# A four-block diffusion backbone on one core: feed-forward parts of 8, 8 and 6 blocks instead of 12 and 10, and a weight ring of four 8 KB slots instead of two of 12 KB

## What is computed

```python
FFN_HIDDEN = ((8 * D_MODEL // 3 + 255) // 256) * 256          # 2816 = 22 blocks of 128

def swiglu(h, w13, w2):
    a, b = jnp.split(h @ w13, 2, axis=-1)
    return (jax.nn.silu(a) * b) @ w2

silu_c = jax.nn.silu(c)
...
for i in range(DEPTH):
    ...
    mod_l = jnp.split((silu_c @ mod_w[i] + mod_b[i])[:, None, :], N_MOD, axis=-1)   # mod_w[i]: 1024 x 6144
    hl = modulate(rmsnorm(xl, mix_pre_g[i]), mod_l[0], mod_l[1])
    ...
```

## Time and profile before

| | |
|---|---|
| median of 3 runs | 2926.69 us (2925.06 to 2929.64) |
| span of the profiled execution | 2911.3 us |
| median less span (what lies around the span) | 15.4 us |
| PE busy | 2446.2 us, 84% |
| DVE, ACT, POOL busy | 1263.4, 773.5, 209.5 us |
| bytes moved | 305.42 MB, 105 GB/s over the span |
| mean granted clock of PE | 0.908 |

### The profile page before, as it was taken

How to read it: one execution, slowest core, us unless ns; L and a number is a source line. 1 busy time by engine, 2 the same in 40 slices (tenths; PEclk the granted TensorE clock), 3 DMA queues, 4 the chain that set the end, 5 groups by cost and what they waited for, 6 DMA issues and landing times.

```text
span 2911.3 us, 29789 instructions
## 1 busy us (share of the span) xinstructions
PE 2446.2 (84%) x12523; PEld 1820.3 (63%) x12523; DVE 1263.4 (43%) x1889; ACT 773.5 (27%) x1225; POOL 209.5 (7%) x167
## 2 busy tenths in 40 slices
PE   7897787999997998989999972617548799998998
PEld 3664463888882774537888821516347399764997
DVE  2333434332325564243313337875741354423545
ACT  1442223222223322133322312200101244302443
POOL 0000000000001001000000022705300000000000
PEclk9997899999999999999999986856658999999999
DMA  5321005332225420153323253100103655445653
GB/s 190 108 70 54 1 30 173 101 128 69 96 83 174 139 73 0 44 175 114 109 80 105 83 146 115 26 4 8 30 0 109 199 193 173 160 153 194 201 171 115
DMA packets 299487, 305.42 MB, mean 105 GB/s; under 512 B 8310, under 2 KB 295745, under 8 KB 299036
## 3 DMA queue, kind: packets, MB, share of 16 engines
q1 hardware_dynamic: 297024, 298.22, 32.0%
q0 software_dynamic: 1616, 5.05, 0.7%
q10 hardware_dynamic: 716, 0.26, 0.0%
HBM read 295.12 MB, written 4.19 MB: 103 GB/s over the span
## 4 chain that ended last, share of the span: by engine, by line
PE 72%; DVE 15%; DMA 6%; ACT 3%; issue 2%; SPq 1%; ACTq 0%; DVEq 0%
PE bank L743 16%; PE bank L744 16%; PE bank L745 16%; PE bank L344 7%; DMA ring<-mod_w 5%; PE bank L646 3%; PE bank L433 2%; PE bank L688 2%; ACT arena L528 1%; PE bank L1379 1%; PE bank L1917 1%; PE bank L1919 1%; PE bank L1918 1%; DVE arena L1748 1%; DVE arena L1751 1%
## 5 line engine op out<-in xcount | busy, mean ns | idle before, releaser
L743 PE MATMUL bank<-h_hi,w_hi 128*128 128x512 f32 (+1 forms) x1480 | 507.8, 343 | 13.4 <-DVE w_lo L723 11.0
L723 DVE TENSOR_TENSOR w_lo<-ring,w_hi 128x1024 fp32r<-128x1024 f32 (+2 forms) x250 | 318.9, 1318 | 459.6 <-ACT w_hi L718 459.6
L744 PE MATMUL bank<-h_lo,w_hi 128*128 128x512 f32 (+1 forms) x1480 | 506.1, 342 | 0.0
L745 PE MATMUL bank<-h_hi,w_lo 128*128 128x512 f32 (+1 forms) x1480 | 505.5, 342 | 0.0
L344 PE MATMUL bank<-ring,silu_c 128*2 128x256 f32 x1536 | 356.1, 390 | 71.8 <-DMA ring<-mod_w 66.8
L344 PEld LDWEIGHTS bank<-ring,silu_c 128*2 128x2 f32 x1536 | 127.5, 87 | 303.7 <-DMA ring<-mod_w 94.7
L743 PEld LDWEIGHTS bank<-h_hi,w_hi 128*128 128x128 f32 x1480 | 284.4, 192 | 46.2 <-DVE w_lo L723 9.5
L744 PEld LDWEIGHTS bank<-h_lo,w_hi 128*128 128x128 f32 x1480 | 284.4, 192 | 31.4 <-issue 0.2
L745 PEld LDWEIGHTS bank<-h_hi,w_lo 128*128 128x128 f32 x1480 | 284.2, 192 | 31.5
L718 ACT ACTIVATE w_hi<-ring 128x1024 fp32r<-128x1024 f32 (+2 forms) x250 | 268.6, 1124 | 17.1 <-DMA ring<-ffn_w 17.1
L743 PE MATMUL bank<-g_hi,w_hi 128*128 128x512 f32 (+1 forms) x704 | 236.5, 336 | 0.0
(11 more groups left out here) (304 smaller groups left out, 3370.9 us busy)
## 6 DMA issues: line engine op xcount, KB each, us to landing
ring<-mod_w SPq DMA_DIRECT2D x96, 1024.0 KB, 5.2
ring<-ffn_w SPq DMA_DIRECT2D x88, 1024.0 KB, 5.1
ring<-ffn_w SPq DMA_DIRECT2D x16, 1536.0 KB, 6.6
ring<-ffn_w SPq DMA_DIRECT2D x16, 1280.0 KB, 5.8
ring<-hy_w_in SPq DMA_DIRECT2D x12, 1024.0 KB, 5.1
ring<-s_w_glu SPq DMA_DIRECT2D x8, 1024.0 KB, 5.4
ring<-mla_w_uq SPq DMA_DIRECT2D x8, 576.0 KB, 4.1
ring<-mla_w_in SPq DMA_DIRECT2D x4, 1024.0 KB, 5.5
```

Of the source, the lines that this page charges most:

```text
L723: nc.vector.tensor_tensor(self.lo[:, i % SPLIT, a:b], self.w.slot(i)[:, a:b], self.hi[:, i % SPLIT, a:b].bitcast(F32), ALU.subtract).then_ ...
L743: nc.tensor.matmul(o, w[0], v[0], start=first, stop=False)
L744: nc.tensor.matmul(o, w[0], v[1], start=False, stop=False)
L745: return nc.tensor.matmul(o, w[1], v[0], start=False, stop=last)
```

## The change

The ring gets four slots of 8 KB for two of 12 KB (32 KB a partition for 24), and the inner blocks are cut 8, 8, 6 instead of 12, 10. A down panel is then at most 8 blocks high, and each feed-forward has three down products: 34 panels for 30, the same matmuls. The middle part's sums are added into `SQ` by DVE (a new step, `ffn_added`). PE's wait at the head of a part is for the last two outputs, one by one, and stands only before kind 0. The semaphores of the four feed-forwards become one set with running counts. `gate_rows` becomes a tile of its own, the arena shrinks, and for this some tiles move: Hyena's `ics` takes a place that is free only after its filter transform, so its load waits for that (`k_summed`, 8); S5's staging tiles go to the tail behind the arena; attention's `mla_q_lo` moves onto `z`, with one wait more on DVE.

```diff
-RING = 2
+RING = 4
 SPLIT = 2
-SLOT = 12 * 256
-UP_CHUNKS = (12, 10)
-ARENA = 32768
+SLOT = KD * 256
+UP_CHUNKS = (8, 8, 6)
+ARENA = 29824
...
-        gate_rows = place("gate_rows", at - D, [D])
+        gate_rows = sb("gate_rows", [P, D])
+        tail = place("tail", KD * TOK + ARENA, [KD * TOK])
...
                         if kind < 2:
                             f = self.f_of(i) + q
-                            if part and c == 0:
-                                pe.wait_ge(self.partial, KD)
+                            if part and c == 0 and kind == 0:
+                                pe.wait_ge(*self.moved(part - 1, KD - 2 + q))
                             if c >= 2:
-                                pe.wait_ge(self.product, f - 1)
+                                pe.wait_ge(ffn_product, self.f0 + f - 1)
...
             def moved(self, part, c):
-                return (self.total, c + 1) if part else (self.partial, c + 1)
+                return ((ffn_partial, ffn_added, ffn_total)[part], KD * self.nth + c + 1)
...
-                        elif kind == 2 and part == 1:
-                            dve.wait_ge(self.summed, 2 * i + q + 1)
-                            dve.wait_ge(self.partial, KD)
+                        elif kind == 2 and 0 < part < self.LAST:
+                            dve.wait_ge(ffn_summed, self.s0 + 2 * i + q + 1)
+                            dve.wait_ge(*self.moved(0, KD - 1))
+                            nc.vector.tensor_tensor(SQ[:, c + q, 0:n], self.out(i, q)[:, 0:n], SQ[:, c + q, 0:n],
+                                                    ALU.add).then_inc(ffn_added, 1)
+                        elif kind == 2 and part == self.LAST:
+                            dve.wait_ge(ffn_summed, self.s0 + 2 * i + q + 1)
+                            dve.wait_ge(*self.moved(self.LAST - 1, KD - 1))
                             nc.vector.tensor_tensor(h[:, c + q, 0:n], self.out(i, q)[:, 0:n], SQ[:, c + q, 0:n],
-                                                    ALU.add).then_inc(self.total, 1)
+                                                    ALU.add).then_inc(ffn_total, 1)
...
+                dve.wait_ge(self.z_split_ready, 6)
                 self.wuq.ahead(self.wuq.remain, dve)
...
+                pool.wait_ge(self.k_summed, 8)
+                pool.dma_start(self.ics, A["k_idft_odd"]).then_inc(self.loaded3, 16)
...
                             pe.wait_ge(self.t_inv, 1)
+                            pe.wait_ge(self.loaded3, 16)
```

More of the change, by code:

```diff
@@ L745, in product @@
             return nc.tensor.matmul(o, w[1], v[0], start=False, stop=last)
+        ffn_summed, ffn_silu, ffn_product = sem("ffn_summed"), sem("ffn_silu"), sem("ffn_product")
+        ffn_g_rounded, ffn_g = sem("ffn_g_rounded"), sem("ffn_g")
+        ffn_partial, ffn_added, ffn_total = sem("ffn_partial"), sem("ffn_added"), sem("ffn_total")
+        n_ffn = [0]
         class Ffn:
+            LAST = len(UP_CHUNKS) - 1
             def __init__(self, layer, n, pre, post):
                 self.n, self.pre, self.post = n, pre, post
-                s = lambda name: sem(f"ffn{layer}_{name}")
-                self.summed, self.silu, self.product, self.g_rounded, self.g = s("summed"), s("silu"), s("product"), s("g_rounded"), s("g")
-                self.partial, self.total = s("partial"), s("total")
+                self.nth = n_ffn[0]
+                n_ffn[0] += 1
+                self.f0 = KF * self.nth
                 self.silus = area(KD * TOK, 2, TOK)
@@ L774, in __init__ @@
                     f0 += nf
-                self.w = Split(loads, [(p[2], 256) for p in self.plan], lambda i: (self.summed, 2 * (i + 1)))
+                self.s0 = 2 * len(self.plan) * self.nth
+                self.w = Split(loads, [(p[2], 256) for p in self.plan], lambda i: (ffn_summed, self.s0 + 2 * (i + 1)))
             def out(self, i, q):
@@ L805, in tensor @@
                             if kind == 2 and c + q == 0:
-                                pe.wait_ge(self.g, sum(UP_CHUNKS[:part]) + k + 1)
+                                pe.wait_ge(ffn_g, self.f0 + sum(UP_CHUNKS[:part]) + k + 1)
                             v_hi, v_lo = (h_hi, h_lo) if kind < 2 else (g_hi, g_lo)
@@ L821, in scalar @@
                         if kind == 0:
-                            act.wait_ge(self.summed, 2 * i + q + 1)
+                            act.wait_ge(ffn_summed, self.s0 + 2 * i + q + 1)
                             if f + q >= 2:
-                                act.wait_ge(self.g, f + q - 1)
-                            nc.scalar.activation(self.silus[:, q, 0:n], self.out(i, q)[:, 0:n], ACT.Silu).then_inc(self.silu, 1)
+                                act.wait_ge(ffn_g, self.f0 + f + q - 1)
+                            nc.scalar.activation(self.silus[:, q, 0:n], self.out(i, q)[:, 0:n], ACT.Silu).then_inc(ffn_silu, 1)
                         elif kind == 1:
-                            act.wait_ge(self.product, f + q + 1)
+                            act.wait_ge(ffn_product, self.f0 + f + q + 1)
                             if part and c == 0 and q == 0:
-                                act.wait_ge(self.partial, KD)
-                            nc.scalar.activation(g_hi[:, c + q, 0:n], self.silus[:, q, 0:n], ACT.Copy).then_inc(self.g_rounded, 1)
+                                act.wait_ge(*self.moved(part - 1, KD - 1))
+                            nc.scalar.activation(g_hi[:, c + q, 0:n], self.silus[:, q, 0:n], ACT.Copy).then_inc(ffn_g_rounded, 1)
                         elif part == 0:
-                            act.wait_ge(self.summed, 2 * i + q + 1)
-                            nc.scalar.activation(SQ[:, c + q, 0:n], self.out(i, q)[:, 0:n], ACT.Copy).then_inc(self.partial, 1)
-                        else:
-                            act.wait_ge(self.total, c + q + 1)
+                            act.wait_ge(ffn_summed, self.s0 + 2 * i + q + 1)
+                            nc.scalar.activation(SQ[:, c + q, 0:n], self.out(i, q)[:, 0:n], ACT.Copy).then_inc(ffn_partial, 1)
+                        elif part == self.LAST:
+                            act.wait_ge(*self.moved(part, c + q))
                             self.post.move(act, c + q, h[:, c + q, :])
@@ L904, in __init__ @@
                 self.q_summed, self.q_moved = sem("mla_q_summed"), sem("mla_q_moved")
-                hi, lo = (place(n, KD * TOK + a, [SPLIT, 6 * 192], F32R) for n, a in (("mla_q_hi", 0), ("mla_q_lo", at + 19776)))
+                hi, lo = (place(n, KD * TOK + a, [SPLIT, 6 * 192], F32R) for n, a in (("mla_q_hi", 0), ("mla_q_lo", KD * TOK)))
                 self.wuq = Split([[cols_of(A["mla_w_uq"][0], i * 192, 192)] for i in range(HEADS)], [(6, 192)] * HEADS,
@@ L1247, in __init__ @@
                 self.cs = area(28672, 2, 2, LAT)
[L1248 to L1249 removed]
+                self.ics = area(7168, 2, 2, LAT)
+                self.loaded, self.loaded2, self.loaded3 = sem("hy_small_loaded"), sem("hy_tables_loaded"), sem("hy_inverse_loaded")
                 self.padded = sem("hy_pads_zeroed")
@@ L1281, in gpsimd @@
                 pool.dma_start(self.cs, A["k_dft_odd"]).then_inc(self.loaded2, 16)
-                pool.dma_start(self.ics, A["k_idft_odd"]).then_inc(self.loaded2, 16)
                 for b in range(2):
```

28 lines of the change are left out of this document (13 added, 15 removed).

## The result

| | before | after |
|---|---|---|
| median (runs, all) | 2927.18 us (4; 2925.06 to 2929.64) | 2848.84 us (4; 2837.0, 2838.68, 2858.99, 2859.57) |
| ratio of after to before | | 0.9732, interval 0.9694 to 0.977 |
| span of the profiled execution | 2911.3 us | 2835.2 us |
| mean granted clock of PE in it | 0.908 | 0.907 |

The change makes the kernel 2.7% faster, 78.3 us by the medians. The direction is right and the size too small: 66.5 us were forecast. The two profiled executions were granted nearly the same clock, so they are compared span against span: 2911.3 - 2835.2 = **76.1 us**.

The account below looks back on a forecast made before the run. PE's matmuls on split weights hold most of the chain, with `mod_w` transfers on the path in the modulation. 52.6 + 3.0 + 8.5 + 2.4 = 66.5 us off the 2911.3 span, plus 15.4 around it, gave 2860.2 us, range 2852 to 2879.

Parts of the forecast that it names:

- The waits in the eight-panel parts: Modulation's eight-panel parts: with four slots all of PE's waits for `mod_w` there go, 52.6 us, all on the path.
- The long stall ahead of S5: Eight-panel part ahead of S5: the 11.47 us wait goes, since its late panel is issued 8.8 us earlier, ahead of S5's loads.
- ahead of S5 1.6: Gate part ahead of S5: most of its 1.80 us wait counts, a gain of 1.6 us, at least 0.7.
- Rival one: Gate panels ahead of S5, or the start: the stall moves there; three late panels cost 5 to 10 us; chance 0.18.
- Clock: Last two panels ahead of S5: the 1.2 GHz clock after the long wait goes with it, 3.0 us.
- fewer slow-clock stretches, such as those at the start of most eight-panel parts: Eight-panel parts: the case of a time better than 2853 us; chance 0.03.
- Heads of the later mixers and feed-forwards: Layers 2 and 3, 256 tokens: FNet's head gains 1.8 us, the feed-forward heads 2.4 and 2.7; 6.9 in all.
- The 512-token gates: Gate parts with 512 tokens: the 1.7 us waits are covered by DVE's norm chain, so nothing is counted.
- Feed-forward: All four feed-forwards: PE's wait at the turn from down to up goes, 2.4 us; the second turn costs nothing.
- the rival that ended slower: Last down product of six blocks: bound by the weights' split on ACT and DVE, eating the whole gain; chance 0.03.
- A deeper wait: Behind the modulation: DVE's or ACT's chain after the post-norm becomes last; half the gain lost, 2893 us; chance 0.05.
- the ring does not run ahead: SP's queue: in-order waits leave two panels in flight, so 2920 us; chance 0.03, shared with gain lost elsewhere.

Follow-up runs that it names:

- e1: The changed kernel with two ring slots for four, all else of the change kept: 2924.59 us, 0.9991 of the kernel before.
- e9: The kernel before, with four small filler products ahead of each of attention's 32 `weigh` steps and nothing of the change: 2912.09 us, 0.9952 of before.
- e10: The changed kernel with two ring slots for four and the filler products in attention: 2907.17 us, 0.9941 of the kernel before.
- e3: The changed kernel with the old wait at a feed-forward part's head, for the last output before either kind of up product: 2860.05 us, 0.9775 of before.
- e4: The changed kernel run again with nothing edited, for its spread: 2855.84 us (2836.53 to 2868.02), 0.9748 of the kernel before.
- e5: The changed kernel with POOL's loads for S5 held until PE is done with layer 2's eight-panel part: 2859.16 us, 0.9758 of before.
- e7: The changed kernel with four small filler products ahead of each of attention's 32 `weigh` steps: 2832.24 us, 0.9671 of the kernel before.

## Why the prediction was right, and where it failed

**The waits in the eight-panel parts: right.** 52.6 us forecast, 52.8 measured. The reading of the earlier trace rows (a period of one landing and one panel) gave both the place and the price, and e1 brings all of it back with one number.

**The long stall ahead of S5: right in the eight-panel part, wrong behind it.** The part went from 47.85 to 29.37 us. But the term "ahead of S5 1.6" of the gate parts came out as +2.5: the last gate panel was the one that landed in S5's loads. Rival one named this, with "one such landing is on record"; the trace now shows that all four gate panels land after 16 to 21 us, and that the room was 18.5 us, not the 14 that I set against it (my own times, issued at 1705 and needed at 1723, gave 18). It came true for one panel of four, with a cost of 4.1 us against the forecast, not 5 to 10.

**Clock: the step that failed.** The prediction's words are: "Without the wait this goes too: 3.0 us", counted for one place, after the one long wait. Measured were 13.0 us of busy time over eight parts. Two parts at clock 1.00 separate the two causes.'s part has three waits and 28.27 us of busy time; the same part after has none and 27.79. So three waits cost 0.48 us in busy time too, 0.16 each. That is what the overlap of neighbouring matmuls is worth: one is recorded for 0.38 us (the median in after), and in an unbroken stretch the next starts after 27.79 / 128 = 0.22. The eight parts have 28 waits ('s 36 less one for each gate part; the prediction's three for each part would be 24), so this makes 4.5 us.

The other 8.5 us are stretches at the low clock: 242.32 - 8 x 27.79 - 4.5 = 15.5 before, 229.32 - 8 x 27.79 = 7.0 after. Of these I had the 3.0 us, and had even listed "fewer slow-clock stretches, such as those at the start of most eight-panel parts" as a case of 3%. The windows of before showed them: clock 0.94 to 0.97 in six of eight parts. I had read the earlier trace rows, whose part is the only one at 1.00, as the pattern for all.

That this isn't a chance of one execution is shown by the other profiles: the busy time of the eight parts is 242.3, 245.7, 248.1 and 243.8 us in the four kernels with two slots (before, e1, e9, e10), and 229.3, 230.5, 234.7, 230.5 and 234.1 in the five with four slots and no filler behind the feed-forwards (after, e3, e4, e5, e7), 245.0 against 231.8 in the mean. e1 (245.7) and e4 (234.7) differ by nothing but the depth. Not all of the low stretches belong to the ring: those at the start of a part behind a feed-forward are there with four slots too. Two others are there with two slots alone. In the first part of before the clock falls just after the second wait, 18.6 us in, and stays low for 3.4 us (timeline, then window):

```profile
39.70 8.76 PE L344 MATMUL bank<-ring,silu_c 128*2 128x256 f32 x32 [2.14 <-DMA ring<-mod_w]
```
```profile
40.33:43.75 3.42, 3.42 (x9) 1.03 (x8) 0.00 (x0) 0.00 (x0) 0.00 (x0) 0.50 0.50 175
```

e9 and e10 have such a stretch at the second wait too, e1 hasn't. And the last part takes 30.1 to 30.5 us of busy time in all four kernels with two slots, and 27.8 in all nine with three or four. Why the clock falls at one break and not at the next is open: the earlier trace rows's part has three breaks and stays at 1.00.

**Heads of the later mixers and feed-forwards: right.** 6.9 us forecast, 8.0 measured. ACT's wait for `ffn_w` is gone: where it stood 6.53 us for the first panel, it now rounds two panels in one stretch while PE works on the gate, and DVE follows, which PE awaits for 1.82 us (timeline of layer 2's head, after):

```profile
2259.90 13.97 PE L345 MATMUL bank<-ring,silu_c 128*2 128x256 f32 x64
...
2270.76 3.88 ACT L719 ACTIVATE w_hi<-ring 128x1024 fp32r<-128x1024 f32 x4
...
2275.60 4.62 DVE L724 TENSOR_TENSOR w_lo<-ring,w_hi 128x1024 fp32r<-128x1024 f32 x4
...
2276.87 0.39 PE L744 MATMUL bank<-h_hi,w_hi 128*128 128x256 f32 x1 [1.82 <-DVE w_lo L724]
```

**The 512-token gates: right at 0.** In layer 0's feed-forward the gate part lost its wait, and the wait for `gate_rows` grew by it, from 4.43 to

```profile
493.30 1.09 PE L356 MATMUL bank<-ident,gate_rows 2*128 2x2 f32 x8 [6.42 <-DVE gate_rows L362]
```

**Feed-forward: direction right, size too small.** Forecast 2.4 us, measured 5.9. The four old waits list 2.3 us; at e3's price for a stop, 0.27 us more for each, they are worth 3.4. The other 2.5 go with the clock at the head of each feed-forward, a second place where the prediction put the clock at nothing. Layer 2's first 6 us, before and after:

```profile
2328.97:2334.97 6.00, 6.00 (x31) 6.00 (x32) 3.44 (x3) 3.67 (x4) 0.00 (x0) 0.57 0.65 208
```
```profile
2276.87:2282.87 6.00, 6.00 (x37) 6.00 (x38) 3.35 (x3) 0.38 (x1) 0.00 (x0) 0.72 0.88 296
```

The four heads have 0.65, 0.58, 0.57 and 0.58 before and 0.70, 0.67, 0.72 and 0.76 after. What is missing to 1.00, times 6 us, sums to 9.7 and 6.9 us: 2.8 less. Why it is less wasn't tried. What I feared didn't come: windows of layer 0's and layer 2's feed-forwards after, and the only wait of PE in each, at its head:

```profile
495.50:860.00 364.50, 361.01 (x1584) 298.50 (x1584) 119.61 (x131) 104.76 (x143) 0.00 (x0) 0.99 0.29 96
2276.00:2470.00 194.00, 191.82 (x1584) 191.62 (x1584) 101.15 (x130) 86.52 (x132) 0.00 (x0) 0.99 0.57 184
```
```profile
PE bank L744 <- DVE w_lo L724: 1.8, 1, 1.8
```

The last down product of six blocks keeps up, so the rival that ended slower had no ground. The start isn't delayed (first modulation panel at 21.58, 21.69 before), and Hyena's `ics` holds nothing up (L1391 waits 4.1 us for DVE, as before). "A deeper wait" and "the ring does not run ahead" did not happen either; e1 is what the latter would have looked like, 2924.59 where I had 2920.

**The conversion, and the range.** "With the 15.4 us that lie around it" is wrong: about 2 us lie around a span, and the rest was that the profiled execution was one of before's shorter ones. It did no harm to the difference, but it hid what mattered for the range: that one kernel's executions differ by up to 31.5 us (e4) with PE's clock. The three listed runs of before lay within 4.6 us; the 47 later ones lie between 2910.77 and 2941.38. Four runs that differ by 22.6 us (after) give a median that is loose by several us, and the forecast range had no term for it, only the bounds of the costs. At the low end it allowed 8 us below the forecast.

So the miss has two parts. The first is the sum: against 66.5 us, 76.1 were measured between the spans. The clock term was 10.0 too small, the feed-forward 3.5, the heads 1.1 and the waits 0.2; against that the gate part ahead of S5 came out 4.1 worse, and Hyena, S5 and the rest, which had no term, 1.1 worse. The second is a range without the spread of the runs.

## What to carry to other kernels

A ring of streamed panels needs enough slots that the work on the panels ahead of it outlasts one landing (here three, with 5.3 us against 3.5). Where other loads share the DMA one slot more helped here, though not wholly: the wait went from 9.96 to 2.66 us. A short wait that repeats costs more than its own length: count the restart (0.16 to 0.27 us here) and read the granted clock of every stretch with such waits, not of the longest alone. Before a range is set, compare the profiled execution's clock and span with the listed runs, because that spread may exceed the disputed costs.

## What the runs showed of the hardware that was not expected

- Waits of about 1.4 us, repeated through attention, go with a granted clock of PE of 0.76 to 0.78 over a stretch of 135 us (260 to 395) in one execution (e4, 35.0 us in 26 waits), and with 0.84 to 0.91 in another of the same kernel (after, 34.8 us in 23). The Trainium skill ("TensorE: Matmul & The Clock Gate", A second HAM failure mode: psum-queue depth-cycling) describes the like for another kernel: short idle moments between groups of matmuls, frequent enough, make the clock swing between its two levels. The trace agrees, and adds its size: 4 filler products for each step restore 0.99 and save 23.6 us of median.
- Filler in attention saves 23.6 us in the changed kernel, but only 13 to 19 us in the kernel before (2912.09 against 2925.25 to 2930.88). I had expected 20 to 25 there. e9's profile has 0.96 in attention (260 to 395), where e7's has 0.99, and its next modulation part ran at 0.88; how much of the difference that is, and why, is open.
- An issue on SP took 8.44 us instead of 0.37, and landings 16.1 to 21.4 us instead of 5.2, while POOL's queue loaded S5's tables. With the loads held back (e5) the landings are 5.2 to 5.4 us. What makes the issue itself long was not tried.
- Low stretches at the start of a part differ between executions at the same idle time just ahead of it (1.45 us in both): the second part of layer 0 took 27.79 us in after and 30.70 in e4. What decides it is open.
